# The split input of the first expert table, moved up 192 bytes in SBUF

## The reference, cut to what matters

```
idx, g = experts and gates that each token's query chooses (8 heads, 16 each)
ue = jnp.take(u_tab, idx, axis=0)
ve = jnp.take(v_tab, idx, axis=0)
act = gelu(einsum('thkd,td->thk', ue, t))
out = einsum('thk,thkd->td', g * act, ve)
```

## Time and profile before

| | us |
|---|---|
| median of 3 runs | 2208.57 |
| lowest and highest | 2206.86, 2210.18 |
| the profiled execution | 2221.41 |
| its span | 2219.6 |
| TensorE busy in it | 2176.5 (98%) |
| VectorE busy | 1695.6 (76%) |
| ScalarE busy | 1310.8 (59%) |
| granted TensorE clock, mean | 0.996 |

### The profile page before, as it was taken

One profiled execution on the slowest core, in us unless ns is written; L12 is line 12 of the kernel. 1 busy time (PEld: TensorE's weight loads), 2 busy tenths in 40 slices (PEclk: granted clock), 3 DMA queues, 4 the chain that ended last, 5 costly groups with the idle time before them and its releaser, 6 DMA issues.

```text
span 2219.6 us, 48312 instructions
## 1 busy us (share of the span) xinstructions
PE 2176.5 (98%) x15536; PEld 2003.8 (90%) x15536; DVE 1695.6 (76%) x3714; ACT 1310.8 (59%) x2733; POOL 433.1 (20%) x277
## 2 busy tenths in 40 slices
PE   8999999999999999999999999999999999999999
PEld 2888899999999888888889989999999998888888
DVE  4787779998789777777656866778888698777777
ACT  3577556656677555555555554665555587555554
POOL 0000005766660000000000000016667620000000
PEclk9999999999999999999999999999999999999999
DMA  8777546777754766666445434557777745666665
GB/s 314 261 242 240 182 149 190 195 194 194 194 143 133 212 213 213 213 213 214 153 162 173 150 106 151 198 160 186 187 184 188 188 124 165 213 213 214 213 213 169
DMA packets 191118, 422.88 MB, mean 191 GB/s; under 512 B 54288, under 2 KB 88336, under 8 KB 190624
## 3 DMA queue, kind: packets, MB, share of 16 engines
q1 hardware_dynamic: 150112, 413.73, 57.4%
q0 software_dynamic: 36864, 0.15, 4.7%
q10 hardware_dynamic: 4032, 7.64, 1.0%
HBM read 403.48 MB, written 17.96 MB: 190 GB/s over the span
## 4 chain that ended last, share of the span: by engine, by line
PE 91%; DVE 3%; ACT 2%; DMA 1%; issue 1%; POOL 0%; DVEq 0%; SPq 0%; ACTq 0%; POOLq 0%
PE ps L2243 21%; PE ps L935 15%; PE ps L937 15%; PE ps L936 15%; PE ps L2244 11%; PE ps L960 5%; PE ps L2593 3%; DMA ring<-stream 1%; PE ps L1866 1%; PE ps L1844 1%; PE ps L2279 1%; PE ps L2166 1%; DVE ring_lo L614 1%; ACT arena L679 1%; PE ps L1858 1%
## 5 line engine op out<-in xcount | busy, mean ns | idle before, releaser
L2243 PE MATMUL ps<-csplit,hl 128*128 128x512 f32 x2048 | 710.4, 392 | 5.5 <-issue 4.5
L2517 POOL DMA_INDIRECT gates<-gbuf,picks_at x256 | 428.5, 1674 | 832.6 <-issue 447.3
L935 PE MATMUL ps<-hsplit,hl 128*128 128x256 f32 x2048 | 573.5, 280 | 0.0
L2244 PE MATMUL ps<-csplit,hl 128*128 128x256 f32 x2048 | 572.0, 279 | 0.0
L936 PE MATMUL ps<-hsplit,hl 128*128 128x256 f32 x2048 | 570.5, 279 | 0.0
L937 PE MATMUL ps<-hsplit,hl 128*128 128x256 f32 x2048 | 570.4, 279 | 0.0
L2323 ACT CAST hl<-ring 128x512 fp32r<-128x512 f32 x562 | 342.2, 620 | 270.3 <-PE ps L937 267.6
L2243 PEld LDWEIGHTS ps<-csplit,hl 128*128 128x128 f32 x2048 | 384.8, 188 | 91.1 <-issue 4.8
L2326 DVE TENSOR_TENSOR hl<-ring,hl 128x512 fp32r<-128x512 f32 x562 | 385.5, 692 | 106.5 <-ACT hl L2323 81.4
L2700 DVE TENSOR_TENSOR hl<-ring,hl 128x512 fp32r<-128x512 f32 x508 | 351.3, 693 | 68.3 <-ACT hl L2690 55.6
L937 PEld LDWEIGHTS ps<-hsplit,hl 128*128 128x128 f32 x2048 | 388.1, 190 | 0.0
(11 more groups left out here) (430 smaller groups left out, 3477.7 us busy)
## 6 DMA issues: line engine op xcount, KB each, us to landing
ring<-stream SPq DMA_DIRECT2D x675, 512.0 KB
s_area<-stream SPq DMA_DIRECT2D x48, 512.0 KB, 5.0
gates<-zeros SPq DMA_DIRECT2D x32, 512.0 KB, 5.0
gring<-gates SPq DMA_DIRECT2D x256, 64.0 KB, 4.1
gates<-gbuf,picks_at POOLq DMA_INDIRECT x256
arena<-xc ACTq DMA_DIRECT2D x2, 1024.0 KB, 15.7
arena<-keys ACTq DMA_DIRECT2D x2, 1024.0 KB, 8.2
gbuf<-consts ACTq DMA_DIRECT2D x1, 1120.0 KB, 5.3
```

What stands on the lines that cost most here:

```text
L935: pe.matmul(out_ap, w[0], m[0], start=start, stop=False)
L2243: pe.matmul(ps[:, bank, :], w_hi, m_both, start=start, stop=False)
L2244: return pe.matmul(ps[:, bank, 0:T], w_lo, m_both[:, 0, :], start=False, stop=stop)
L2517: pool.indirect_dma_start(out=cells, out_offset=bass.IndirectOffsetOnAxis(ap=picks_at[:, i, c:c + 1], axis=0), in_=gates[:, i, c:c + 1], i ...
```

## The change

`hsplit` begins 96 words instead of 48 behind the end of `hl`, at byte 193024, which is 512 modulo 1024 (before 192832, 320 modulo 1024). The reservation ahead of the small tables grows by the same 48 words, so that `picks_best`, `gates`, `pos_f`, `rank1`, `rank2`, `key_f`, `chosen`, `gate_sum`, `picks_pos`, `picks_key`, `picks_at` and `late` all move up by 192 bytes. `csplit`, `h1_parts`, `mixed_parts` and `raw_split` keep `SHIFT` = 48.

```diff
     SHIFT = 48
-    hsplit, _ = place("hsplit", [P, 2, KD, T], F32R, at=gbuf_at + 2 * HLRING * HALF + SHIFT)
+    U_SHIFT = 96
+    hsplit, _ = place("hsplit", [P, 2, KD, T], F32R, at=gbuf_at + 2 * HLRING * HALF + U_SHIFT)
     cpair, _ = place("csplit", [P, CRING, 2, T + SHIFT], F32R, at=gbuf_at + 2 * HLRING * HALF)
...
     K = Space(gbuf, 10240)
-    K.take(8192 + SHIFT)
+    K.take(8192 + max(SHIFT, U_SHIFT))
```

## The result

| | before | after |
|---|---|---|
| median | 2209.38 (4 runs, 2206.86 to 2221.96) | 2237.31 (4 runs, 2233.64 to 2242.14) |
| the profiled execution | 2221.41 | 2240.60 |
| its span | 2219.6 | 2238.8 |

All times are in us. The change made the kernel slower: the ratio is 1.0118, with a 95% interval from 1.0092 to 1.0144. The prediction said 2218 us, with a range of 2200 to 2237; the measured time lies at its upper end.

What follows compares the result with a forecast made beforehand. The prediction took the distance between TensorE matmul starts in the first tables as the bound: 0.117 us, +0.035 us x 256 units = +8.9 us on 2208.6, forecast 2218 us, range 2200 to 2237.

Steps and rivals of the forecast that it cites:

- second branch: Timed runs before short in both layers, 2.72 us per unit: the change costs 22.5 us, giving 2231 us.
- first branch: Timed runs before mixed like the profile, 0.1156 us mean distance: the change costs 8.9 us, giving 2217.5 us.
- The bound: First-table stretches of both layers: TensorE always busy, so only the distance between matmul starts counts; VectorE has slack.
- The side: First-table triples: the new offset lengthens the distance; slower by over 0.2% (4.4 us) was given 0.56.
- The distance: First-table matmuls at the new offset: 0.117 us between starts, chosen between 0.118 (n_hi projections) and 0.115 (second table).
- cqn: Projection with moving rows and weights at equal offsets, starts 0.120 us apart; taken as the distance's long end.
- The base: Old timed median 2208.6 us, 12.8 us below the profiled execution; the gap was taken as the profiler's own cost.
- The rhythms: First-table triples: two distances at one address pair, 0.113 and 0.118 us per matmul; a disturbance of the stream flips them.
- Parts (2) and (3): Small tables 192 bytes higher cost nothing; csplit does not move, so the second table is untouched.
- A: First-table triples: distance independent of the offset, the same two rhythms, no change at 2208.6 us; chance 0.18.
- B: First-table triples: short rhythm taken in both layers, 13.7 us faster, 2195 us, or 2202 in part; chance 0.26.
- C: First-table triples: pattern repeats every 128 bytes, all at 0.120 us, 2236 us or 2250; chance 0.13.

Runs made afterwards that it cites:

- all_moved: Kernel before with gbuf and everything placed behind it 192 bytes higher, hsplit still 192 bytes from the weights: 2217.25 us, ratio 0.9997.
- same_again: The kernel before, unchanged, timed and profiled again: 2219.98 us, ratio 1.0009; its profiled execution took 2209.39 us.
- set_short: Kernel before plus nine extra matmuls ahead of unit 3 of each layer's first table, the last 256 columns wide: 2210.66 us, ratio 0.9963.
- set_long: Kernel before plus nine extra matmuls ahead of unit 3 of each layer's first table, the last 258 columns wide: 2229.92 us, ratio 1.0038.
- tables_only: Kernel before with only the small tables 192 bytes higher, hsplit unmoved: 2218.15 us, ratio 1.0005.
- off128: Kernel before with hsplit 128 bytes behind hl's end, small tables as in the changed kernel: 2235.59 us, ratio 1.0094.
- off64: Kernel before with hsplit 64 bytes behind the weights, small tables as in the changed kernel: 2231.93 us, ratio 1.0071.
- off0: Kernel before with hsplit at the weights' own offset modulo 512, small tables as in the changed kernel: 2242.30 us, ratio 1.0117.
- funnel_map: Kernel before plus eleven extra matmuls ahead of units 3, 106 and 112 to 127 of each layer, last width varied: 2251.62 us in a single run.
- off224: Kernel before with hsplit 224 bytes behind the weights, small tables as in the changed kernel: 2234.96 us, ratio 1.0083.

## Why the prediction was right and where it was wrong

**The number.** The measured 2237.3 us lies at the edge of the range, and the step was larger than forecast: 9 us were forecast, 28 came out against the runs shown ahead of it and 18 against all 87. Two steps of the prediction were low, the distance and the base. That the time still came out at the range's end owes something to luck: the second branch of the prediction's own sum, taken with its own upper bound of 0.120 us, gives 2250, and the range left that out. The forecast's own range of 2213 to 2231 doesn't follow from its distances either: 0.1156 to 0.1185 us over 6144 matmuls is 2208.6 to 2226.4 on the first branch and 2222.7 to 2240.5 on the second.

**The bound.** Right. The distance between starts on TensorE is the time; VectorE became less busy (234.52 of 270 us in the first stretch, 243.55 in the earlier trace rows) and ended no wait of TensorE.

**The side.** Right: the offset changed, the counts fell, the kernel became slower. all_moved shows that it is the offset and not hsplit's address.

**The distance.** This step failed in size. I took 0.117 us between the row from n_hi and that of the second table; measured are 118.6 and 120.0 ns, so that one layer sits at the upper bound from cqn. The 0.115 of the second table is a bad neighbour: there a 512-column matmul stands between, as the prediction itself said, and it should then not have pulled the value down. The row of n_hi averages over four offsets, so it too holds the new one only in part. The row with the same shape and a single offset was cqn; that one of the two rhythms at offset 128 would have just its distance could not be known before.

**The base.** This step failed too, and it explains more of the difference, 13 of the 19 us between 2218 and 2237. The forecast rested on timed runs as mixed as the profile and put the 12.8 us between them down to the profiler. same_again ran 12.0 us quicker than the first profile, as a profile, with both layers short. So for the three runs shown the second branch of the sum held: 2.72 us per unit before. Over all 87 runs before is mixed, as the first branch has it, but then its median is 2219 and not 2208.6; the forecast took the mixed distance from the one and the low time from the other. The second branch gave 2231 at the 0.117. With the distances measured by count and its own way of counting all 256 units it would have given 2208.6 + 24 x 128 x (5.4 + 6.6) ns = 2245; the sum over 106 units alone gives 2239.2, and 2237.3 was measured. The 22 last units of each layer do take part, but less than that way of counting says, since about half of them ran at the long distance before. From the first start of unit 106 to the last start of the stage it is 91.67 us in each layer of after, against 90.45 and 89.93 in same_again, 3.0 us in all and not 6.3. The second tables give that back: they take 354.9 us each, against 356.5 and 356.4. The rest of the kernel differs by 1 us between the two profiles.

**The rhythms.** Right, and the larger find. Two rhythms at one offset and a disturbance that picks one of them: set_short and set_long put a layer into either by two columns of one matmul, as far as the profiles and most of the timed runs show.

**Parts (2) and (3).** Right: tables_only changes nothing, and the second table starts 955 in 330 us before and after. I did not foresee the 1.6 us at its start in the profiled pair.

**The rivals.** A (no change) falls: at offset 128 neither the 795 nor the 765 of offset 192 was seen in the profiles of after and off128. The prediction had the Trainium skill (page "SBUF — State Buffer", section "Who interferes with whom") on this side: its two read ports of PE are independent, and PE never waits on anyone. That section is about engines that hold one another up, and in this stream TensorE stands behind no other engine. What does not hold for this stream is the conclusion that a start address therefore changes nothing: TensorE starts between 750 and 795 of the same triples in 270 us at clock 1.00, depending on where the moving row lies and on which rhythm it takes there. That the two reads collide at a port is not shown; the runs show the distance, not its cause. B (faster) falls. C came nearest: its 0.120 is what the second layer does, and the time lies beside its lower price of 2236. Its reason is wrong all the same: the pattern doesn't repeat every 128 bytes (off64), and the first layer runs at 118.6. Its higher price of 2250, for all units at 0.120, is 8 us above what off0 measured with exactly that distance. Most of that is again the 22 last units, which cost 3.2 us more in off0 than in same_again and not 7.0, and the second tables, which take 3.0 us less. I had argued against C from single steps of the second table, which proved right on the period and wrong on the time: another period doesn't keep the distance from being long.

**What stays open.** Why the layers of after took 118.6 and 120.0, whether an execution can swap them (its four runs lie in two pairs, at 2234 and at 2241), and what inside the chip makes the pattern.

## What to carry to other kernels

When matmuls stand back to back with a weight load each and the engine is busy all the time, count starts per stretch and not durations: the offset between the moving row and the weights can cost 6% of such a stretch, and the value has to be measured for the shape at hand. If a kernel's runs fall into groups a fixed distance apart, look for a rhythm that changes between executions before trusting three runs or one profile as a base, and compare counts of each stage as well as medians. Where the start of a long stretch decides which rhythm it takes, a few matmuls ahead of it may hold the good one for 2 us: set_short did in all of 12 runs, while set_long, with the other rhythm, seems to have missed in 4 of 12.

## What the runs showed of the hardware

The distance of the starts of 256-column triples, by offset: 120.0 ns at 0; 117.6 at 64; 118.6 or 120.0 at 128; 118.6 or 117.2 at 160; 113.2 or 117.6 at 192; 118.3 at 224. Only 192 had the short one, in the profiles taken.

A rhythm held for over 100 units when nothing came between. In funnel_map both layers agree after each of the 18 runs of matmuls at offset 0, though they came to the first of them in different rhythms; in set_long 4 of 12 executions lie about 10 us below the others, so whether this holds in every execution is open.

At the start of a second table the granted clock was 0.66 in the 5 us after idle times of 2.16 us (before, layer 1) and 1.77 us (off224, layer 2), and 1.00 after 1.61 us (after, layer 1) and 2.29 us (before, layer 2): the length of the idle time alone does not decide it.
